# Reciprocal of the deviation in PSUM, another bank for a mean's rest, and rearranged last sums in two middle layer norms

## The reference, cut to what matters

```python
def _layer_norm(x, g, b):
    mu = jnp.mean(xf, axis=-1, keepdims=True)
    var = jnp.mean(jnp.square(xf - mu), axis=-1, keepdims=True)
    return ((xf - mu) * lax.rsqrt(var + LN_EPS) * g + b).astype(x.dtype)

h = _layer_norm(DEEPNORM_ALPHA * h + mixed, ln1_g[l], ln1_b[l])                        # norm 1
h = _layer_norm(DEEPNORM_ALPHA * h + _memory_cross_attention(h, mem, ...), ln2_g[l], ln2_b[l])   # norm 2
h = _layer_norm(DEEPNORM_ALPHA * h + _swiglu(h, ffn_w_in[l], ffn_w_out[l]), ln3_g[l], ln3_b[l])
```

## Time and profile before

| | |
|---|---|
| median of 3 runs | 1173.4 us (1172.08 to 1174.16) |
| the profiled execution | 1173.72 us |
| its span, first to last instruction | 1171.9 us |
| mean granted clock of TensorE in it | 0.988 |
| TensorE busy | 1131.0 us, 97% |
| DVE / ACT / POOL busy | 537.9 / 436.2 / 504.1 us |

### The profile page before, as it was taken

One profiled execution on the slowest core, in us unless ns is written; L12 is line 12 of the kernel. 1 busy time (PEld: TensorE's weight loads), 2 busy tenths in 40 slices (PEclk: granted clock), 3 DMA queues, 4 the chain that ended last, 5 costly groups with the idle time before them and its releaser, 6 DMA issues.

```text
span 1171.9 us, 16854 instructions
## 1 busy us (share of the span) xinstructions
PE 1131.0 (97%) x6109; PEld 907.9 (77%) x6109; DVE 537.9 (46%) x1121; ACT 436.2 (37%) x766; POOL 504.1 (43%) x320
## 2 busy tenths in 40 slices
PE   6999999999999999999999899989999999999996
PEld 6878888887885666668887686767888888888885
DVE  7999912320147666656445716465323222210005
ACT  4341333321247666753333614236232232321211
POOL 5641442441133444555555640336444444434442
PEclk9998999999999999999999999998999999999999
DMA  6742331773121000013343330122333333223222
GB/s 191 95 104 69 95 103 51 237 176 74 37 73 36 1 2 2 2 55 107 97 133 125 114 107 19 58 86 91 107 89 99 98 90 107 89 73 103 95 91 89
DMA packets 158384, 101.68 MB, mean 87 GB/s; under 512 B 18344, under 2 KB 145968, under 8 KB 158192
## 3 DMA queue, kind: packets, MB, share of 16 engines
q1 hardware_dynamic: 153408, 94.48, 28.8%
q10 hardware_dynamic: 4912, 6.35, 1.6%
HBM read 93.59 MB, written 2.10 MB: 82 GB/s over the span
## 4 chain that ended last, share of the span: by engine, by line
PE 82%; DVE 6%; issue 4%; POOL 4%; ACT 2%; DMA 1%; POOLq 0%; SPq 0%; DVEq 0%; ACTq 0%
PE bank L1395 78%; PE bank L1710 3%; POOL wlo L822 2%; DVE xc L891 1%; DVE Sr L1205 1%; POOL hLo L836 1%; DVE st L1375 0%; DVE bnst L910 0%; DVE xmax L1336 0%; DMA wraw<-in_xattn_w_kv 0%; ACT hHi L538 0%; ACT Wst L609 0%; DMA xtok<-in_x 0%; DVE xPT L1350 0%; DVE rstd L1291 0%
## 5 line engine op out<-in xcount | busy, mean ns | idle before, releaser
L822 POOL TENSOR_TENSOR wlo<-wraw,whi 128x1024 fp32r<-128x1024 f32 x160 | 394.0, 2464 | 521.7 <-ACT whi L498 521.5
L498 ACT ACTIVATE whi<-wraw 128x1024 fp32r<-128x1024 f32 x160 | 169.4, 1060 | 556.0 <-PE bank L1395 207.4
L1395 PE MATMUL bank<-hHi,whi 128*128 128x512 f32 x736 | 291.6, 396 | 10.8 <-ACT hHi L538 6.8
L1395 PE MATMUL bank<-hHi,wlo 128*128 128x512 f32 x736 | 289.6, 394 | 0.0
L1395 PE MATMUL bank<-hLo,whi 128*128 128x512 f32 x736 | 284.2, 391 | 0.0
L1395 PEld LDWEIGHTS bank<-hHi,whi 128*128 128x128 f32 x736 | 140.4, 191 | 42.3 <-ACT hHi L538 7.6
L1395 PEld LDWEIGHTS bank<-hHi,wlo 128*128 128x128 f32 x736 | 140.0, 190 | 29.7
L1395 PEld LDWEIGHTS bank<-hLo,whi 128*128 128x128 f32 x736 | 139.2, 189 | 28.5
L862 POOL TENSOR_SCALAR Sr<-Sr,winv,gates 128x512 f32<-128x512 f32 (+3 forms) x128 | 76.5, 607 | 78.6 <-DVE winv L1216 78.5
L891 DVE TENSOR_TENSOR sLo<-sF,sHi 128x512 f32 x22 | 50.1, 2276 | 97.7 <-ACT sHi L764 97.7
L683 ACT ACTIVATE Sr<-Sr,nmax 128x512 f32<-128x512 f32 (+3 forms) x128 | 71.7, 560 | 43.9 <-DVE nmax L1205 42.1
(11 more groups left out here) (314 smaller groups left out, 1736.3 us busy)
## 6 DMA issues: line engine op xcount, KB each, us to landing
wraw<-in_ffn_w_in SPq DMA_DIRECT2D x88, 256.0 KB, 3.2
wraw<-in_w_in SPq DMA_DIRECT2D x80, 256.0 KB, 3.4
wraw<-in_ffn_w_out SPq DMA_DIRECT2D x44, 256.0 KB, 2.7
wraw<-in_xattn_w_kv SPq DMA_DIRECT2D x32, 256.0 KB, 3.1
w<-in_cmp_w ACTq DMA_DIRECT2D x1, 4096.0 KB, 20.2
wraw<-in_nsa_w_out SPq DMA_DIRECT2D x16, 256.0 KB, 3.1
wraw<-in_w_out SPq DMA_DIRECT2D x16, 256.0 KB, 3.1
wraw<-in_xattn_w_q SPq DMA_DIRECT2D x16, 256.0 KB, 3.1
```

The lines of the kernel that those rows point to most:

```text
L498: act.activation(hi_of(c)[:, :], wraw[c % 4][:, :], ACT.Copy).then_inc(w_hi_ready, 1)
L822: pool.tensor_tensor(wlo[c % 4][:, :], wraw[c % 4][:, :], hi_of(c)[:, :].bitcast(F32), ALU.subtract).then_inc(w_lo_ready, 1)
L1395: return pe.matmul(o, w, a, start=start, stop=stop)
```

## The change

1. The reciprocal of the deviation is written to bank 7 of PSUM and no longer over `rstd` in SBUF; the sixteen multiplications (eight in each norm) read it from there. Bank 7 held the variance, which is read before.
2. The delta of norm 1 goes to bank 6, which held the first mean, and no longer to bank 0. The wait for all eight recentrings ahead of xq is taken out.
3. On ACT in norm 1, the pair hHi[0], hF[0] comes ahead of the split of block b0 + 5, and each later split comes one pair later, the one of b0 + 9 behind m = 5.
4. In norm 2, DVE no longer adds xc[7] to `hsum`; TensorE multiplies xc[7] by `mean_w` itself, as a second product into the delta. For this DVE adds sq of tile 6 to `ssum`, which TensorE did as a product of its own.

```diff
-DELTA_BANK = (0, 5)
+DELTA_BANK = (6, 5)
...
             split(b0 + 4)
-            split(b0 + 5)
             for m in range(KT):
                 h_hi(act, 1, m, 16)
-                if m in (0, 1, 2):
-                    split(b0 + 6 + m)
-                elif m == 4:
+                if m < 4:
+                    split(b0 + 5 + m)
+                elif m == 5:
                     split(b0 + 9)
...
-                if t >= 5:
+                if t >= 5 and (n, t) != (2, 7):
                     dve.wait_ge(xc_ready, KT * (n - 1) + t + 1)
...
-                for m in {5: (1, 2, 3), 6: (4, 5)}.get(t, ()):
+                for m in {5: (1, 2, 3), 6: (4, 5) if n == 1 else (4, 5, 6)}.get(t, ()):
...
-                link(dve.reciprocal(rstd[:, :], rstd[:, :]))
+                link(dve.reciprocal(bank[7][:, :], rstd[:, :]))
                 for m in range(KT):
                     dve.wait_ge(ctr_ready, KT * (n - 1) + m + 1)
-                    tt(xc[:, m, :], xc[:, m, :], rstd[:, :], ALU.mult).then_inc(nrm_ready, 1)
+                    tt(xc[:, m, :], xc[:, m, :], bank[7][:, :], ALU.mult).then_inc(nrm_ready, 1)
...
-                pe.wait_ge(ssum_ready, 5 * n)
+                delta = bank[DELTA_BANK[n - 1]][:, :]
+                pe.wait_ge(ssum_ready, 5 if n == 1 else 11)
                 mm(bank[7][:, :], mean_w[:, :], ssum[:, :], True, False)
-                pe.wait_ge(sq_ready, KT * (n - 1) + 7)
-                mm(bank[7][:, :], mean_w[:, :], sq[2][:, :], False, False)
-                pe.wait_ge(delta_sum, 3 * n)
-                mm(bank[DELTA_BANK[n - 1]][:, :], mean_w[:, :], hsum[:, :], True, True).then_inc(delta_ready, 1)
+                if n == 1:
...
+                else:
+                    pe.wait_ge(delta_sum, 5)
+                    mm(delta, mean_w[:, :], hsum[:, :], True, False)
+                    pe.wait_ge(xc_ready, 2 * KT)
+                    mm(delta, mean_w[:, :], xc[:, 7, :], False, True).then_inc(delta_ready, 1)
...
-            pe.wait_ge(ctr_ready, KT)
             tile_stage("xq", hHi, hLo, tile_dve, TD["xq"], made=lambda k: (hlo_ready, KT + k + 1))
```

More of the change, by code:

```diff
@@ L1750, in variance @@
             def variance(n):
-                pe.wait_ge(ssum_ready, 5 * n)
+                delta = bank[DELTA_BANK[n - 1]][:, :]
+                pe.wait_ge(ssum_ready, 5 if n == 1 else 11)
                 mm(bank[7][:, :], mean_w[:, :], ssum[:, :], True, False)
-                pe.wait_ge(sq_ready, KT * (n - 1) + 7)
-                mm(bank[7][:, :], mean_w[:, :], sq[2][:, :], False, False)
-                pe.wait_ge(delta_sum, 3 * n)
-                mm(bank[DELTA_BANK[n - 1]][:, :], mean_w[:, :], hsum[:, :], True, True).then_inc(delta_ready, 1)
+                if n == 1:
+                    pe.wait_ge(sq_ready, 7)
+                    mm(bank[7][:, :], mean_w[:, :], sq[2][:, :], False, False)
+                    pe.wait_ge(delta_sum, 3)
+                    mm(delta, mean_w[:, :], hsum[:, :], True, True).then_inc(delta_ready, 1)
+                else:
[3 more added lines that the diff above has]
+                    mm(delta, mean_w[:, :], xc[:, 7, :], False, True).then_inc(delta_ready, 1)
                 pe.wait_ge(sq_ready, KT * n)
```

## The result

| | before | changed |
|---|---|---|
| median, first comparison | 1173.2 us (6 runs) | 1167.9 us (6 runs, 1166.9 to 1168.1) |
| the profiled execution | 1173.7 | 1168.1 |
| its span | 1171.9 | 1166.3 |
| mean granted clock | 0.988 | 0.991 |

The ratio is 0.9941, with a 95% interval of 0.9912 to 0.9969: faster by 5.3 us, between 3.6 and 10. The median of before moves between comparisons; over 35 executions in the first experiments it was 1172.6, which makes the gain 4.7. The profiled execution of before lies some 1.1 us above that median. Some 15 to 20 in a hundred executions of most kernels here, before included, are about 8 us longer than the others, and they raise a kernel's median the more of them it has (most in e8, four of twelve) and widen the intervals.

What follows compares the result with a forecast made beforehand. TensorE was taken to bound the kernel, so time was only to be had where it stands still or runs below full clock. Norm 1's 3.3, norm 2's 1.1 and the clock's 0.3 made 4.7: 1169.0 us, range 1166.3 to 1171.9.

Steps and rivals of the forecast that it cites:

- the clock term: After TensorE's restart in norm 2: a shorter wait shortens the half-clock stretch, saving 0 to 1.3 us, taken as 0.3.
- Norm 1, the sum: First xq tile behind norm 1 ends at 663.4 rather than 666.7, a gain of 3.3 us.
- Norm 1, the causes: Norm 1's 3.3 us come from unblocked multiplications, hHi 0 ahead of a split, and the removed wait for recentrings.
- Norm 2: Last sums of norm 2: the delta is complete at 785.1 instead of 786.25, 1.1 us earlier, and TensorE restarts at 792.75.
- Reciprocal into PSUM: DVE's reciprocal written to bank 7 in both norms: 0 us extra, with a range of 0 to 2.2.
- Rival D: The reciprocal's write into PSUM costs extra, making the kernel slower; 1175.5 us if its duration doubles; chance 0.05.
- 62 cycles more for a PSUM source: Documented extra for each of the sixteen multiplications, 0.065 us, making the gain 0.13 smaller; left out of the forecast.
- A: The forecast as worked out for both norms: 1169.0 us, own range 1168 to 1170.4; chance 0.50.
- B: In norm 1 DVE gets ahead of POOL, the xq tile runs unbroken: gain 6.5, 1167.2 us; chance 0.25.
- C: Norm 1 gains nothing, multiplications still blocked or hLo eating the gain; 1.1 to 1.8 us remain, 1171.9; chance 0.19.

Runs made afterwards that it cites:

- the first experiments: The comparison in which e1, e2, e3 and e4 were timed against the kernel before, whose median there was 1172.6 us.
- e8: Changed kernel with norm 2's reciprocal back in SBUF, norm 1's still in bank 7; median 1169.0 us against 1172.9 for before, ratio 0.9963.
- e2: Kernel before with only norm 2's last sums rearranged; median 1171.9 us against 1172.6 for before, ratio 1.0002.
- e6: Changed kernel with ACT's split of xq block 1 behind pair m = 6 instead of m = 5; median 1168.5 us against 1172.9 for before, ratio 0.9963.
- e4: Changed kernel with ACT's old order in norm 1; median 1167.8 us against 1172.6 for before, ratio 0.9963.
- e5: Changed kernel with TensorE's wait for all eight recentrings put back ahead of xq; median 1168.4 us against 1172.9 for before, ratio 0.9964.
- e1: Kernel before with only the reciprocal in PSUM bank 7 and the multiplications reading it, both norms; median 1170.0 us against 1172.6, ratio 0.9977.
- e3: Kernel before with only norm 1's delta in bank 6, no wait for recentrings and ACT's new order; median 1173.4 us against 1172.6, ratio 1.0008.
- e9: Kernel before with 11 unread filling products in norm 1 ahead of the wait for recentrings; median 1172.8 us against 1172.9, ratio 1.0.

## Why the prediction was right or wrong, point by point

- **Total.** Forecast 1169.0, a gain of 4.7 which I subtracted from the profiled 1173.7. Measured: median 1167.9, the profiled execution 1168.1, which is 5.65 by the spans. The direction and the range were right, the likeliest value was 1.1 us high.
- **The step that failed is the clock term.** I took 0.3 out of "0 to 1.3", with no row that gave its length. In the profiled pair it was 0.97, and of the 0.95 by which that pair's gain exceeds the forecast 0.67 lie here and 0.26 in norm 1; the 0.15 left of the 1.1 is the median's distance from the profiled execution. The 0.97 is not a property of the change: e2, with the same sums, had the long stretch again, and e6 almost. That larger groups give a gain of 4.7 (4.8 in e4, 4.5 and 4.4 in e5 and e6), in which such stretches average out, is not to the credit of the 0.3, which was a guess.
- **Norm 1, the sum.** 3.3 forecast, 3.56 measured in the pair. The slots were right: four hLo blocked by four low parts, hLo 4 by the fifth, multiplications of 0.68, the order of hLo and multiplications as worked out, waits of 0.85, 0.24 and a small one against 1.1, 0.4 and 0.3, and full clock. About half of the 0.26 is the start of POOL's work: I left the split of block b0 + 5 at 643.91, as if its load had to land as late as in before, but it ran at 643.66 without waiting for it, so POOL's low parts came at 644.78 rather than 645.05 and the fifth at 656.57 rather than 656.85. The other half is the second tile of before, which starts at 666.81, not 666.7.
- **Norm 1, the causes.** Here the mechanism was wrong in part: the prediction gave credit to steps that earn nothing. It had hHi 0 ahead of a split, and the end of the wait for the recentrings, as conditions of the gain. e1 has neither and gains at least as much; e3 has both and gains nothing; e4 and e5 undo them one at a time without loss. My own schedule could have told: nothing in it waited for ACT before m = 5, and the last recentring ends there ahead of 655.
- **Norm 2.** 1.1 forecast, 1.11 measured. But I expected a remaining wait for hHi of 5.7. It stayed at 6.78: the saved time was TensorE's other wait, the 0.90 ahead of the hsum product, together with 0.2 of issue and product. The added ssum step was hidden as said: DVE still had 0.72 us of idleness ahead of the last residual, and the xc product followed at 0.86.
- **Reciprocal into PSUM.** 0 forecast with a bound of 2.2; measured 3.36 against 3.35. Rival D falls.
- **62 cycles more for a PSUM source.** The Trainium skill, page "VectorE: DVE Perf Modes", section "The TRN2 errata", would add an estimated 0.065 us to every multiplication. Fourteen operations at a mean of 0.676 against 0.679 for the fastest multiplication of before, with two SBUF operands, leave no room for it: the measurement decides. The lock that the Trainium skill describes, page "SBUF — State Buffer", section "SBUF: two separate sides", is borne out by e1, where the multiplications with an operand in PSUM are at 0.677, by e3, where those with two in SBUF are at a mean of 1.235, and by e6, where hLo 4 takes 0.68 instead of 2.80 once POOL's instruction is moved away.
- **Rivals of the prediction.** A was the case that came, a little below its own range of 1168 to 1170.4. B (DVE ahead of POOL) came in neither race, by margins of 0.32 and 0.16 us. C, that the multiplications stay blocked, is refuted by their 0.676. C was also added up wrongly: what would have remained of the gain, 1.1 to 1.8, gives 1171.9 to 1172.6, so the range took in only its edge, and none of it lies below 1171.05, where I counted a third.

## What to carry to other kernels

Where DVE and POOL work at the same time, look at which operand of a DVE operation is used over and over: put into PSUM, here, it freed all the elementwise operations that read it from waiting for POOL (0.676 us against a mean of 1.509), at no cost in their duration. Then count POOL's slots, for what stays with two SBUF operands still went at one per POOL instruction, and moving an instruction in POOL's order only made it block the next (e6). Where the matrix engine must wait several microseconds for a known chain, products that nobody reads kept its clock up here, and they paid only where the engine itself, and not that chain, limits what follows: 2.1 to 2.6 us in norm 2, nothing in norm 1. And where a load lands at a slightly different time in each execution, compare one stretch over several traces before a tenth of a microsecond is put down to an edit.

## What the runs showed of the hardware that was not expected

- After the same wait of 6.8 us, the lower clock lasted between 3.8 us (the changed kernel, e3, e4, e5) and 6.2 us (e2) from the restart, in ten traces. A single profiled pair can differ by a microsecond for that alone.
- TensorE can also have the lower clock while it is busy. In the profiled executions of e8 and e9 the window below lies in the last part of the attention, where its matmuls are small (64 x 128 and 128 x 128); before had 1.00 there, with TensorE busy for 19.13 us of the 20. Norm 1's reciprocal starts at 645.73 in e8 and at 646.41 in e9, 7.6 and 8.3 us later than in before. What starts it stays open. The row is e8's:

```profile
500.00:520.00 20.00, 20.00 (x112) 11.79 (x110) 9.63 (x61) 10.15 (x43) 7.87 (x18) 0.50 0.00 1
```
